# Triangular inverse of the gated delta rule: blocks up to 32 turned by VectorE, corrections masked where they are written, products copied by ScalarE

## The reference, cut to what matters

```python
lower = jnp.where(strict, jnp.einsum('bhnid,bhnjd->bhnij', kb, k) * decay, 0.0)
a_mat = lower + jnp.eye(C, dtype=f32)
rhs = jnp.concatenate([vb, kb * jnp.exp(gc)[..., None]], axis=-1)
sol = lax.linalg.triangular_solve(a_mat, rhs, left_side=True, lower=True, unit_diagonal=True)
...
def step(S, xs):
    q_i, attn_i, u_i, w_i, k_i, gl_i = xs
    v_new = u_i - jnp.einsum('bhcd,bhde->bhce', w_i, S)
    o = jnp.einsum('bhcd,bhde->bhce', q_i, S) + jnp.einsum('bhij,bhje->bhie', attn_i, v_new)
    S = S * jnp.exp(gl_i)[..., None, None] + jnp.einsum('bhcd,bhce->bhde', k_i, v_new)
    return S, o
```

## Time and profile before

| | |
|---|---|
| median of 3 runs (lowest to highest) | 2087.7 us (2085.82 to 2089.68) |
| the profiled execution's own time | 2088.97 us |
| its span in the profile | 2087.2 us |
| the pairs and levels (stage from 983 to 1165 us) | 182 us |
| PE busy in that stage | 167.81 us |
| DVE busy in that stage | 124.75 us |
| ACT busy in that stage | 79.95 us |

### The profile page before, as it was taken

One profiled execution on the slowest core, in us unless ns is written; L12 is line 12 of the kernel. 1 busy time (PEld: TensorE's weight loads), 2 busy tenths in 40 slices (PEclk: granted clock), 3 DMA queues, 4 the chain that ended last, 5 costly groups with the idle time before them and its releaser, 6 DMA issues.

```text
span 2087.2 us, 27694 instructions
## 1 busy us (share of the span) xinstructions
PE 2011.4 (96%) x10454; PEld 1699.9 (81%) x10454; DVE 1123.3 (54%) x1365; ACT 952.3 (46%) x1322; POOL 288.1 (14%) x435
## 2 busy tenths in 40 slices
PE   7999999999999999997999899998999999999994
PEld 7988888888888888886999787886888888888872
DVE  5105742102231313222677768436988888888875
ACT  5223322213345333312344545212788877777762
POOL 0000000021323232100000000001222222222210
PEclk9999999999999999999999999998999999999997
DMA  4211223242445444226223284326899999999966
GB/s 177 88 55 61 81 81 142 112 161 99 163 147 169 151 158 152 103 109 207 97 81 123 66 315 139 131 81 227 308 377 381 390 392 387 388 387 381 378 232 246
DMA packets 131384, 413.44 MB, mean 198 GB/s; under 512 B 16656, under 2 KB 37856, under 8 KB 125405
## 3 DMA queue, kind: packets, MB, share of 16 engines
q1 hardware_dynamic: 107308, 351.90, 44.8%
q0 software_dynamic: 23984, 60.26, 8.6%
HBM read 351.05 MB, written 77.82 MB: 205 GB/s over the span
## 4 chain that ended last, share of the span: by engine, by line
PE 88%; DVE 5%; issue 3%; ACT 2%; DMA 2%; POOL 0%; SPq 0%; DVEq 0%; POOLq 0%; ACTq 0%
PE psum L609 24%; PE psum L611 24%; PE psum L610 24%; PE psum L2336 2%; PE psum L2321 2%; PE psum L2227 1%; PE psum L2205 1%; PE psum L2556 1%; PE psum L2213 1%; DVE e_l L1980 1%; PE psum L2480 1%; PE psum L2176 1%; PE psum L2578 1%; PE psum L2616 1%; PE psum L2617 1%
## 5 line engine op out<-in xcount | busy, mean ns | idle before, releaser
L1980 DVE TENSOR_TENSOR e_l<-e_raw,e_h 128x2048 fp32r<-128x2048 f32 x190 | 423.9, 2287 | 32.4 <-ACT e_h L1283 32.3
L609 PE MATMUL psum<-hT_h,w_l 128*128 128x512 f32 x1088 | 431.9, 397 | 0.0
L611 PE MATMUL psum<-hT_h,w_h 128*128 128x512 f32 x1088 | 424.3, 390 | 0.0
L610 PE MATMUL psum<-hT_l,w_h 128*128 128x512 f32 x1088 | 423.7, 389 | 0.0
L1283 ACT CAST e_h<-e_raw 128x2048 fp32r<-128x2048 f32 x190 | 355.2, 1929 | 29.4 <-DMA e_raw<-in_w_e 25.4
L1409 DVE TENSOR_TENSOR w_l<-wraw,w_h 128x2048 fp32r<-128x2048 f32 (+1 forms) x38 | 87.0, 2290 | 287.6 <-ACT w_h L977 287.6
L611 PEld LDWEIGHTS psum<-hT_h,w_h 128*128 128x128 f32 x1088 | 204.2, 188 | 43.7
L610 PEld LDWEIGHTS psum<-hT_l,w_h 128*128 128x128 f32 x1088 | 204.6, 188 | 40.1
L609 PEld LDWEIGHTS psum<-hT_h,w_l 128*128 128x128 f32 x1088 | 204.5, 188 | 39.7
L609 PE MATMUL psum<-e_h,xT_l 128*128 128x512 f32 x512 | 202.9, 396 | 1.4 <-DVE xT_l L1986 1.4
L611 PE MATMUL psum<-e_h,xT_h 128*128 128x512 f32 x512 | 200.4, 391 | 0.0
(11 more groups left out here) (388 smaller groups left out, 3396.5 us busy)
## 6 DMA issues: line engine op xcount, KB each, us to landing
e_raw<-in_w_e SPq DMA_DIRECT2D x192, 1024.0 KB, 10.7
wraw<-in_w_in_t SPq DMA_DIRECT2D x37, 1024.0 KB, 4.9
pt_scratch<-stage SPq DMA_DIRECT2D x52, 512.0 KB, 2.6
gate<-pt_scratch SPq DMA_DIRECT2D x24, 512.0 KB, 3.7
rows<-rows_scratch SPq DMA_DIRECT2D x8, 1280.0 KB, 8.9
h_scratch<-xn SPq DMA_DIRECT2D x16, 512.0 KB, 3.6
yg<-expert_rows SPq DMA_DIRECT2D x16, 512.0 KB, 10.3
c_all<-attention_scratch POOLq DMA_DIRECT2D x4, 1560.0 KB, 10.1
```

Source lines behind the costliest of these rows:

```text
L609: nc.tensor.matmul(out_ap, ll, rh, start=first, stop=False)
L610: nc.tensor.matmul(out_ap, lh, rl, start=False, stop=False)
L611: return nc.tensor.matmul(out_ap, lh, rh, start=False, stop=last)
L1980: nv.tensor_tensor(e_l[:, c], e_raw[:, c], e_h[:, c].bitcast(F32), ALU.subtract).then_inc(s_el13 if c < 4 else s_el2, 1)
```

## The change

At levels 1 to 5 the blocks of `Di` are no larger than 32, and so is the part to be turned: the 32x32 blocks of `Di` transposed each in its place give the whole transposed matrix. There `inverse_transposed` and `r_out` go, and VectorE transposes `Di` straight into `Ri` (`turned`), behind the two `corrected` of the level before (behind `first_inverse` for level 1). The product is not masked any more: ScalarE copies it whole to `Pm` (`p_out`), and the mask is applied where the correction is written, by a copy under a predicate into `Di`. So that the entries can be copied and need not be subtracted, the lower matrix is built with its sign turned (`kbn` is scaled by -1). `first_inverse` becomes an identity that ScalarE copies into `Di` ahead of time (`identity`) and one predicated copy in place of a multiplication and an addition. Level 6 keeps its TensorE transposes, its masking on VectorE and its copy on ScalarE; its update is an addition now.

```diff
+            def identity(t):
+                if t >= 4:
+                    act.wait_ge(s_x, 12 * ((t - 4) // 2) + 11 + t % 2)
+                nc.scalar.copy(Di[:, t % 4], bheads(ident[:])).then_inc(s_di, 1)
+
+            def p_out(i, l, u):
+                act.wait_ge(s_pp, 12 * i + 2 * (l - 1) + u + 1)
+                nc.scalar.copy(Pm[:, u], banks4(u)).then_inc(s_p, 1)
...
                 for l in range(1, LEVELS):
                     for u in range(2):
-                        r_out(i, l, u)
+                        if l < LEVELS - 1:
+                            p_out(i, l, u)
+                        else:
+                            r_out(i, u)
+                    if l in (1, 2) and c < NT:
+                        identity(c + l - 1)
...
-                    nv.tensor_tensor(SMr[:, :, ROW_KB:ROW_KB + NH], qr[:, :, NH:NQ], beta, ALU.mult)
+                    nv.scalar_tensor_tensor(SMr[:, :, ROW_KB:ROW_KB + NH], qr[:, :, NH:NQ], -1.0, beta, ALU.mult, ALU.mult)
...
             def first_inverse(t):
                 b = 6 if t == 1 else 4
                 dve.wait_ge(s_lt, t + 1)
-                cd.link(nv.tensor_tensor(Di[:, t % 4], banks4(b), bheads(b_lev[:, 1]), ALU.mult))
-                nv.tensor_tensor(Di[:, t % 4], Di[:, t % 4], bheads(ident[:]), ALU.add).then_inc(s_d1, 1)
-
-            def masked(i, l, u):
-                dve.wait_ge(s_pp, 12 * i + 2 * (l - 1) + u + 1)
-                nv.tensor_tensor(Pm[:, u], banks4(u), bheads(b_lev[:, 1 + l]), ALU.mult).then_inc(s_p, 1)
+                dve.wait_ge(s_di, t + 1)
+                nv.copy_predicated(Di[:, t % 4], bheads(b_lev[:, 1]).bitcast(I32), banks4(b)).then_inc(s_d1, 1)
+
+            def turned(i, l, u):
+                t = 2 * i + u
+                if l == 1:
+                    dve.wait_ge(s_d1, t + 1)
+                else:
+                    dve.wait_ge(s_d, 12 * i + 2 * (l - 2) + u + 1)
+                nv.transpose(Ri[:, t % 4], Di[:, t % 4]).then_inc(s_r, 1)
...
             def corrected(i, l, u):
+                t = 2 * i + u
                 dve.wait_ge(s_x, 12 * i + 2 * (l - 1) + u + 1)
-                o = Di[:, (2 * i + u) % 4] if l < LEVELS - 1 else Ri[:, (2 * i + u) % 4]
-                nv.tensor_tensor(o, o, banks4(u), ALU.subtract).then_inc(s_d, 1)
+                if l < LEVELS - 1:
+                    nv.copy_predicated(Di[:, t % 4], bheads(b_lev[:, 1 + l]).bitcast(I32), banks4(u)).then_inc(s_d, 1)
+                else:
+                    nv.tensor_tensor(Ri[:, t % 4], Ri[:, t % 4], banks4(u), ALU.add).then_inc(s_d, 1)
...
                     for u in range(2):
                         corrected(i, l, u)
+                    if l < LEVELS - 2:
+                        for u in range(2):
+                            turned(i, l + 1, u)
...
                     for u in range(2):
                         level_product(i, l, u)
-                    for u in range(2):
-                        inverse_transposed(i, l, u)
+                    if l == LEVELS - 1:
+                        for u in range(2):
+                            inverse_transposed(i, u)
```

More of the change, by code:

```diff
@@ L389, in build @@
         s_pp = sem("level_product")
-        s_tr = sem("inverse_transposed")
-        s_p = sem("level_product_masked")
-        s_r = sem("inverse_transposed_out")
+        s_di = sem("inverse_is_identity")
+        s_tr = sem("last_inverse_transposed")
+        s_p = sem("level_product_out")
+        s_r = sem("inverse_turned")
+        s_p6 = sem("last_level_product_masked")
+        s_r6 = sem("last_inverse_transposed_out")
         s_x = sem("level_correction")
@@ L1155, in kv_scaled, with r_out @@
                 ins.then_inc(s_kd, 1)
-            def r_out(i, l, u):
-                act.wait_ge(s_tr, 12 * i + 2 * (l - 1) + u + 1)
-                nc.scalar.copy(Ri[:, (2 * i + u) % 4], banks4(2 + u)).then_inc(s_r, 1)
+            def identity(t):
[5 more added lines that the diff above has]
+                nc.scalar.copy(Pm[:, u], banks4(u)).then_inc(s_p, 1)
+            def r_out(i, u):
+                act.wait_ge(s_tr, 2 * i + u + 1)
+                nc.scalar.copy(Ri[:, (2 * i + u) % 4], banks4(2 + u)).then_inc(s_r6, 1)
             def vn_out(t):
@@ L1216, in _ @@
             for t in range(2):
+                identity(t)
+            for t in range(2):
                 b_exp(t)
@@ L1634, in first_inverse, with masked @@
                 dve.wait_ge(s_lt, t + 1)
-                cd.link(nv.tensor_tensor(Di[:, t % 4], banks4(b), bheads(b_lev[:, 1]), ALU.mult))
-                nv.tensor_tensor(Di[:, t % 4], Di[:, t % 4], bheads(ident[:]), ALU.add).then_inc(s_d1, 1)
-            def masked(i, l, u):
-                dve.wait_ge(s_pp, 12 * i + 2 * (l - 1) + u + 1)
-                nv.tensor_tensor(Pm[:, u], banks4(u), bheads(b_lev[:, 1 + l]), ALU.mult).then_inc(s_p, 1)
+                dve.wait_ge(s_di, t + 1)
[7 more added lines that the diff above has]
+                nv.transpose(Ri[:, t % 4], Di[:, t % 4]).then_inc(s_r, 1)
+            def masked(i, u):
+                dve.wait_ge(s_pp, 12 * i + 11 + u)
+                nv.tensor_tensor(Pm[:, u], banks4(u), bheads(b_lev[:, LEVELS]), ALU.mult).then_inc(s_p6, 1)
             def corrected(i, l, u):
+                t = 2 * i + u
                 dve.wait_ge(s_x, 12 * i + 2 * (l - 1) + u + 1)
-                o = Di[:, (2 * i + u) % 4] if l < LEVELS - 1 else Ri[:, (2 * i + u) % 4]
-                nv.tensor_tensor(o, o, banks4(u), ALU.subtract).then_inc(s_d, 1)
+                if l < LEVELS - 1:
+                    nv.copy_predicated(Di[:, t % 4], bheads(b_lev[:, 1 + l]).bitcast(I32), banks4(u)).then_inc(s_d, 1)
+                else:
+                    nv.tensor_tensor(Ri[:, t % 4], Ri[:, t % 4], banks4(u), ALU.add).then_inc(s_d, 1)
             def values(t):
@@ L1725, in _ @@
                 first_inverse(t)
+                turned(0, 1, t)
             key_query(2, 0)
@@ L1729, in _ @@
                 for l in range(1, LEVELS):
-                    for u in range(2):
-                        masked(i, l, u)
+                    if l == LEVELS - 1:
+                        for u in range(2):
+                            masked(i, u)
                     if l == 1:
@@ L1754, in _ @@
                             first_inverse(c)
+                            turned(i + 1, 1, 0)
                             key_query(c, 3)
@@ L1764, in _ @@
                             first_inverse(c + 1)
+                            turned(i + 1, 1, 1)
                         if p >= 0:
@@ L2322, in level_product, with inverse_transposed @@
                 ins.then_inc(s_pp, 1)
-            def inverse_transposed(i, l, u):
+            def inverse_transposed(i, u):
                 t = 2 * i + u
@@ L2330, in level_correction @@
             def level_correction(i, l, u):
-                t, n = 2 * i + u, 12 * i + 2 * (l - 1) + u + 1
-                pe.wait_ge(s_p, n)
-                pe.wait_ge(s_r, n)
+                t, n = 2 * i + u, 10 * i + 2 * (l - 1) + u + 1
+                if l < LEVELS - 1:
+                    pe.wait_ge(s_p, n)
+                    pe.wait_ge(s_r, n)
+                else:
+                    pe.wait_ge(s_p6, t + 1)
+                    pe.wait_ge(s_r6, t + 1)
                 for h in range(NH):
@@ L2628, in delta_masks @@
         m = (a // (2 * n) == b // (2 * n)) & (a // n % 2 == 1) & (b // n % 2 == 0)
-        masks.append(np.where(m, 1.0 if l else -1.0, 0.0))
+        masks.append(np.where(m, 1.0, 0.0))
     return np.ascontiguousarray(np.stack(masks, axis=1).astype(np.float32))
```

## The result

| | before | after |
|---|---|---|
| median (lowest to highest), us | 2087.59 (2085.82 to 2089.68) | 2068.21 (2066.77 to 2068.99) |
| the profiled execution's own time, us | 2088.97 | 2068.00 |
| span, us | 2087.2 | 2065.9 |

What follows compares the result with a forecast made beforehand. TensorE was taken as the bound, busy for 96% of the span. Gains in the four pairs, 6.2 + 6.2 + 4.7 + 3.6 = 20.7 us, off 2088.97 gave 2068.3, so a median of 2067; range 2062 to 2079 us.

Steps and rivals of the forecast that it cites:

- The chain on TensorE, shortened by 0.87 us a level: At levels 1 to 5, two tile transposes take 0.87 us of TensorE's queue; 20 x 0.87 = 17.4 us.
- The new operations at 0.69 us: VectorE's transpose and predicated copy were each taken at 0.69 us, like a multiplication of the same shape.
- (A): VectorE's new operations are dear: at 1.28 us a transpose, 13 of 20.7 us gone, 2080 in all; chance 0.12.
- (C): VectorE becomes the bound: gain gone at 1.47 us a transpose; at 1.8 us, 13 us slower, 2101; chance 0.04.
- Second and third pair, 6.2 us each: Levels of the second and third pairs of tiles: shorter by 6.2 us in each pair, summed level by level.
- the half slow stretch of 0.8 us: Second and third pairs, level 4: of 1.6 us lost to slow-clock products behind TensorE's gap, half, 0.8, counted as gained.
- First pair, 4.7 us: First pair: level 1's wait ends 3.6 us earlier, less 0.8 for slow products, plus 1.9 in levels 2 to 5.
- rival (B): The clock: if each gap left on TensorE brings slow products in full, 5 us go, 2072; chance 0.08.
- One sign named for a wrong prediction: A granted TensorE clock of 0.5 to 0.6 filling stretches that had 1.00 before.
- Last pair, 3.6 us: Last pair, without preparation: levels gain 3.8 us as waits for the transposes' copy go; ScalarE's chain lets through 3.6.
- All that follows shifts: Behind the levels, TensorE has no gap in the expert stage, so everything following moves earlier by the same time.
- Rival (D), hidden anyway: TensorE only waits where it transposed, for casts, `tv` or `S`, so nothing is gained: 2088; chance 0.04.

Runs made afterwards that it cites:

- the filled kernel: Changed kernel with products nobody reads put into TensorE's gaps in the first pair's levels 1 and 4 and the next two pairs' level 4: 2063.59 us, ratio 0.9884.
- three such moves: Changed kernel with the load's wait behind the corrections, first inverse ahead of `kbn`, and last pair's casts earlier, no unread products: 2058.44 us, ratio 0.9862.
- the repeated run: The changed kernel measured once more, unaltered, on the chip of the runs with all three reorderings: 2067.92 us, ratio 0.9910.

## Why the prediction was right

**The chain on TensorE, shortened by 0.87 us a level: held.** Put back alone, the transposes cost exactly this in every level of the second pair but the fourth. What the working left unsaid is the condition. It opened the sum with TensorE's 17.4 us, but with the masks kept, and VectorE doing both, only 4 of 19.4 us are gained, and with TensorE's transposes kept 11.5. The replay of each level had both edits in it, and so came out right; the first line of it would not have.

**The new operations at 0.69 us: held** (0.690 and 0.734), so rivals (A) and (C) fell by their condition. Their price was tested: doubled transposes cost 11.4 us, with 2.9 us in the second pair where (A) had 3.2.

**Second and third pair, 6.2 us each: 6.8 and 7.0.** Level by level the second pair gained 0.9, 0.9, 0.9, 3.0, 1.2 and 0.0 us, where the working had 1.1, 0.87, 0.87, 2.24 (1.44 and 0.8), 1.1 and 0. The term that was short is the half slow stretch of 0.8 us that I kept behind level 4: the gap of 1.41 us (1.35 forecast) brought none. In the profile after, by stretch, behind the first pair's gap of 2.29 us and behind this one:

```profile
1007.70:1013.10 5.40, 5.36 (x32) 5.28 (x32) 1.95 (x3) 0.00 (x0) 0.00 (x0) 0.68 0.52 152
1047.70:1051.40 3.70, 3.67 (x33) 3.70 (x34) 1.92 (x3) 0.42 (x2) 0.00 (x0) 1.00 0.27 76
```

**First pair, 4.7 us: 2.3.** The step that was mis-sized is the clock again, the other way. The second level did start 3.9 us earlier (990.35 for 994.22; 3.6 forecast), 0.4 of it because the load landed at 988.35 and not at 988.72, after this chain:

```profile
980.26 8.09 DMA rows<-rows_scratch
...
990.35 2.72 PE psum L2358 x16
```

Without slow stretches levels 2 to 5 would have gained 1.9, as forecast. But two slow stretches of 1.63 us each lie in them, by the filled kernel, where I had taken off 0.8 for the first and nothing for the second. From start to start of the levels that is 3.7 + 1.9 - 3.3 = 2.3. The reason for taking off nothing in level 4 was that this pair's gap of 2.1 us there had brought none before; the gap of 2.29 us brought one. And the gap that rival (B) put at 2.0 us in level 1 was 3.58, since TensorE is now through with its correction early and waits for the load. One sign named for a wrong prediction did come, in this one place: a granted clock of 0.68 behind the gap in level 4, where the products had run at full speed before.

So rival (B) held in the first pair and its opposite in the next two. The forecast counted 2.7 us of clock in its 20.7 (1.9 less 0.8 in the first pair, 0.8 in each of the next two), and the traces show 1.6. That the sum is closer than its terms is in part luck: 2.4 us too much in the first pair against 1.8 too little in the other three. The sum of the pairs is 20.1 us.

**Last pair, 3.6 us: 3.9**, with ScalarE late in levels 4 and 5 as told; TensorE waited 0.84 and 0.65 us for `Pm`. The levels gained 0.9, 1.4, 0.9, 0.35, 0.5 and 0.0, where 0.8, 1.4, 0.9, 0.3 and 0.4 were told.

**All that follows shifts: held**, with the expert stage at 200 of 200 us again. Rival (D), hidden anyway, fell: the transposes put back cost 7.9 us.

## What to carry to other kernels

Where two engines pass a chain back and forth, replay one period with every instruction that stands in each queue, and cost the edits together: moving an operation off the bound engine gave 4 us while the other engine kept its part of the exchange too, and 19 with that gone. An instruction that waits, or that nobody waits for yet, should not stand ahead of one that the chain needs; three such moves brought another 9.5 us with no work removed, a third of them by slow stretches that went. And a gap of some 2 us on TensorE cost another 1.6 us behind it in several places here, so look at the granted clock behind each gap before a saving is read off two profiles.

## What the runs showed that I had not expected

The same gap does not always bring the slow stretch. TensorE in order of time behind the first pair's wait in level 4, first the changed kernel:

```profile
1007.74 1.25 PE L2319 MATMUL psum<-qn,kn 128*128 128x128 f32 x8 [2.29 <-DVE Di L1655]
1008.78 1.92 PE L2327 MATMUL psum<-kbn,kn 128*128 128x128 f32 x8
```

The changed kernel in the repeated run, same view:

```profile
1006.98 1.64 PE L2319 MATMUL psum<-qn,kn 128*128 128x128 f32 x8 [2.29 <-DVE Di L1655]
1008.42 1.91 PE L2327 MATMUL psum<-kbn,kn 128*128 128x128 f32 x8
```

And the kernel with the casts moved in the last pair, whose order is the same at this place:

```profile
1005.99 1.13 PE L2319 MATMUL psum<-qn,kn 128*128 128x128 f32 x8 [2.30 <-DVE Di L1655]
1006.96 1.06 PE L2327 MATMUL psum<-kbn,kn 128*128 128x128 f32 x8
```

In the first the products slow down about 1 us after the gap's end, in the second about 0.5 us, and in the third not at all. In the levels of these runs, gaps of 3.3 us and more were followed by a slow stretch each time, gaps of 1.9 to 2.6 us in some, and those of 1.8 us and less in none. What decides it in between stays open. Products that nobody reads, put into the gap, prevented it: by the medians 4.2 us in the kernel before and 4.6 in the changed one, by the levels 4.9 and 3.3.
